# A seventh slot for weights, with three engines that prepare them one unit further on

## The reference

```
for layer in range(2):
    h = rmsnorm(x, g[0])
    m = mixer_ab(h, ...) if layer % 2 == 0 else mixer_cd(h, ...)
    x = x + rmsnorm(m, g[1])
    x = x + rmsnorm(cross_attn(rmsnorm(x, g[2]), mem, wq, wkv, wo), g[3])
    x = x + rmsnorm(sq_relu_mlp(rmsnorm(x, g[4]), w1, w2), g[5])

def mixer_cd(h, w_in, ...):               # layer 1
    u = h @ w_in                          # 5 x 1024 columns: a, gate, bg, cg, hh
    v = causal_dwconv(a * sigmoid(gate), dw_w) + dw_b       # 31 taps
    conf_out = silu(layernorm(v))
    sc_out = bg * causal_dwconv(cg * hh, sc_w)              # 3 taps
    return concat([conf_out, sc_out]) @ w_out
```

## Time and profile before

| | us |
|---|---|
| median of 3 runs | 913.75 (913.74 to 916.39) |
| profiled execution | 913.8, span 912.1 |
| PE busy | 882.5 (97% of the span) |
| DVE busy | 622.3 (68%) |
| ACT busy | 478.3 (52%) |
| POOL busy | 176.6 (19%) |

### The profile page before, as it was taken

One profiled execution on the slowest core, in us unless ns is written; L12 is line 12 of the kernel. 1 busy time (PEld: TensorE's weight loads), 2 busy tenths in 40 slices (PEclk: granted clock), 3 DMA queues, 4 the chain that ended last, 5 costly groups with the idle time before them and its releaser, 6 DMA issues.

```text
span 912.1 us, 14743 instructions
## 1 busy us (share of the span) xinstructions
PE 882.5 (97%) x6078; PEld 803.3 (88%) x6078; DVE 622.3 (68%) x960; ACT 478.3 (52%) x696; POOL 176.6 (19%) x163
## 2 busy tenths in 40 slices
PE   8999998999999999999998999999998899999997
PEld 8899986898899999998898998887997798999996
DVE  5886996586487555555579999956685565555554
ACT  6754654565465444444564443347664555444443
POOL 1120800000000000000019887666000000000000
PEclk9999999999999999999999999999999999999999
DMA  8554434544465555555556676255542456655551
GB/s 297 164 169 133 140 131 145 171 153 143 149 184 188 187 193 187 185 186 186 183 162 186 194 211 201 95 183 162 172 144 82 136 189 211 192 189 188 185 186 69
DMA packets 82955, 155.27 MB, mean 170 GB/s; under 512 B 6839, under 2 KB 8777, under 8 KB 82889
## 3 DMA queue, kind: packets, MB, share of 16 engines
q1 hardware_dynamic: 82776, 154.29, 52.2%
q10 hardware_dynamic: 112, 0.05, 0.0%
HBM read 152.11 MB, written 1.05 MB: 168 GB/s over the span
## 4 chain that ended last, share of the span: by engine, by line
PE 76%; DVE 13%; ACT 4%; POOL 2%; DMA 1%; SPq 1%; issue 1%; DVEq 0%; POOLq 0%; ACTq 0%
PE ps L556 13%; PE ps L558 13%; PE ps L557 13%; PE ps L623 10%; PE ps L625 10%; PE ps L624 10%; DVE w_lo L1499 4%; DVE ps L1839 2%; ACT w_hi L1094 1%; DVE cv L2018 1%; POOL w_lo L2142 1%; PE ps L681 1%; DVE xT L1778 1%; DMA raw<-in_ab_w_in 1%; DVE xc L1566 1%
## 5 line engine op out<-in xcount | busy, mean ns | idle before, releaser
L1094 ACT ACTIVATE w_hi<-raw 128x1024 fp32r<-128x1024 f32 x284 | 295.4, 1054 | 223.6 <-DMA raw<-in_mlp_w 135.9
L1499 DVE TENSOR_TENSOR w_lo<-raw,w_hi 128x1024 fp32r<-128x1024 f32 x238 | 287.1, 1227 | 129.0 <-ACT w_hi L1094 128.4
L556 PE MATMUL ps<-h_hi,w_hi 128*128 128x256 f32 x1120 | 315.7, 282 | 9.8 <-POOL w_lo L2142 5.9
L558 PE MATMUL ps<-h_hi,w_lo 128*128 128x256 f32 x1120 | 313.3, 280 | 0.0
L557 PE MATMUL ps<-h_lo,w_hi 128*128 128x256 f32 x1120 | 313.3, 280 | 0.0
L556 PEld LDWEIGHTS ps<-h_hi,w_hi 128*128 128x128 f32 x1120 | 212.0, 189 | 13.1 <-POOL w_lo L2142 6.6
L558 PEld LDWEIGHTS ps<-h_hi,w_lo 128*128 128x128 f32 x1120 | 213.2, 190 | 0.0
L557 PEld LDWEIGHTS ps<-h_lo,w_hi 128*128 128x128 f32 x1120 | 211.8, 189 | 0.6
L2171 POOL TENSOR_TENSOR rfac<-stat,mhalf 128x1 f32<-128x1 f32 (+2 forms) x18 | 16.6, 923 | 632.9 <-DVE stat L1752 515.4
L2142 POOL TENSOR_TENSOR w_lo<-raw,w_hi 128x1024 fp32r<-128x1024 f32 x46 | 114.6, 2516 | 23.1 <-ACT w_hi L1094 23.1
L623 PE MATMUL ps<-w_hi,r_hi 128*128 128x512 f32 x256 | 101.0, 395 | 0.0
(11 more groups left out here) (270 smaller groups left out, 1241.8 us busy)
## 6 DMA issues: line engine op xcount, KB each, us to landing
raw<-in_mlp_w SPq DMA_DIRECT2D x128, 512.0 KB, 3.7
raw<-in_cd_w_in SPq DMA_DIRECT2D x40, 512.0 KB, 3.9
raw<-in_xa_wkv SPq DMA_DIRECT2D x32, 512.0 KB, 3.7
raw<-in_ab_w_in SPq DMA_DIRECT2D x24, 512.0 KB, 4.6
raw<-in_xa_wq SPq DMA_DIRECT2D x16, 512.0 KB, 3.6
raw<-in_xa_wo SPq DMA_DIRECT2D x16, 512.0 KB, 3.7
raw<-in_cd_w_out SPq DMA_DIRECT2D x16, 512.0 KB, 3.5
raw<-in_ab_w_out SPq DMA_DIRECT2D x12, 512.0 KB, 3.4
```

The lines of the kernel that those rows point to most:

```text
L556: nc.tensor.matmul(dst, wt[0], x[0], start=start, stop=False, skip_group_check=True)
L558: return nc.tensor.matmul(dst, wt[1], x[0], start=False, stop=stop, skip_group_check=True)
L1094: nc.scalar.activation(w_hi[:, v % SLOTS, :, :], raw[:, v % SLOTS, :, :], ACT.Copy)\
L1499: V.tensor_tensor(w_lo[:, v % SLOTS, :, :], raw[:, v % SLOTS, :, :], f(w_hi[:, v % SLOTS, :, :]), ALU.subtract).then_inc(lo_ready_dve, 1)
```

## The change

SLOTS becomes 7, and the three while loops, on ACT, DVE and POOL, go one unit further than the number in the call for all calls from unit 7 on. [...] The places of the calls aren't edited. `v_at`, from which SP issues its copies of v, contains SLOTS and moves by one unit with it.

```
 P = 128
-SLOTS = 6
+SLOTS = 7
+AHEAD = 1
...
             def round_to(u):
 
-                while nu[0] <= min(u, NU - 1):
+                while nu[0] <= min(u + AHEAD if u >= SLOTS else u, NU - 1):
...
             def low_to(u):
 
-                while nu[0] <= min(u, NU - 1):
+                while nu[0] <= min(u + AHEAD if u >= SLOTS else u, NU - 1):
                     v = nu[0]
                     if not pool_lo[v]:
...
             def low_to(u):
 
-                while nu[0] <= min(u, NU - 1):
+                while nu[0] <= min(u + AHEAD if u >= SLOTS else u, NU - 1):
                     v = nu[0]
                     if pool_lo[v]:
...
-        nc = bacc.Bacc("TRN2", target_bir_lowering=False, num_devices=1)
+        nc = bacc.Bacc("TRN2", target_bir_lowering=False, num_devices=1, dynamic_dma_scratch_size=8192)
```

## The result

The changed kernel is slower: 918.82 us (median of 20 runs, 912.82 to 923.68) against 914.79 us (20 runs, 910.93 to 919.24) on the same chips. The ratio is 1.0046, with a 95% interval of 1.0029 to 1.0063. The profiled execution took 917.85 us, its span is 916.1 us (before 912.1), its mean granted clock 0.991 of full (before 0.994).

The account below looks back on a forecast made before the run. The prediction took TensorE, busy in 97% of the span, as the bound. It summed 1.3 us at the start and 4.5 in layer 1's projections to 5.8, so 913.8 became 908.0 us, with an 8-in-10 range of 904.9 to 911.3.

Parts of the forecast that it names:

- The start, 1.3 us: 0 to 136 us: TensorE's early waits shrink, but VectorE sets the pace; worth VectorE's lead, 1.3 us, between 0 and 3.7.
- The three therefore do the same work at the same moments and wait the same: Whole kernel: ScalarE, VectorE and GpSimd keep their timing; TensorE alone gains, a margin of 2.76 us.
- The waits near 480 us: Layer 1's projections: TensorE waits 0.9 us for unit 148, 1.0 for 149, then runs some 0.6 us ahead of before.
- The 1.38 us wait at 543.33 goes entirely: Layer 1's projections: the margin of 2.76 us removes this TensorE wait, leaving it 2.0 us ahead.
- 3.4 us ahead: Layer 1's projections, before 568.08: units 178/179 come earlier, 2.6 + 0.8 us, with about 1 us of wait left.
- The cap, 3.35 us of slack at S: End of layer 1's projections: VectorE's second sum, with at most 1.3 us of its own gain, caps the stage at 4.3 to 4.7 us.
- The clock fall at 569.5 gone: Layer 1's projections: TensorE's clock no longer falls after the shortened wait, 1.7 us more, 5.1 in all before the limit.
- The rest: From 600 us on: waits of 2.32 us at 691.30 and 3.23 us at 721.95 stay; no gain.
- The rival "slower": 476 to 596 us: VectorE meets GpSimd more often, 2.98 us per newly held group of taps; four give 919.8 us; chance 0.05.

Follow-up runs that it names:

- slots7_only: The kernel before with seven slots and the small scratch, every engine taking its units at the old places: 909.61 us, ratio 0.9949.
- dve_as_before: The changed kernel, but VectorE takes no unit further in the calls for units 140 to 199: 917.21 us, ratio 1.0060.
- pool_yields: The changed kernel, but GpSimd waits for VectorE's low part of unit u-1 before beginning its own of unit u: 912.48 us, ratio 0.9979.

## Why the prediction was wrong, step by step

- *The start, 1.3 us*: right in the first trace, 1.6 us at 478 us, and the new wait for cbm stands where it was named. In the second trace nothing of it is left: VectorE reaches Rsq at 474.24 us, before at 474.22. And the gain was put down to the two parts of the change together; the slot alone gives 2.2 us.
- *"The three therefore do the same work at the same moments and wait the same"*: this step failed. It holds for an engine that handles every unit. But VectorE and GpSimd share the units here, and with each call one unit further VectorE's own unit moves to an earlier call: that of 159 stood behind six taps at 507.00 and stands ahead of them at 503.76, and GpSimd's runs shift as well. What VectorE and GpSimd then hold each other up by was priced at nothing in the sum. It measured 7.2 us in low parts and 2.1 in ml in the profiled execution, 3.1 and 2.1 in the second trace. VectorE's chain grew by 8.4 and 4.4 us.
- *The waits near 480 us*: two of 0.9 and 1.0 us said, 0.76 and 1.55 found, so that the gain of 0.6 us didn't come. The second counted 1.28 us for GpSimd's multiplication of sg between the two low parts; that took 2.28, with VectorE's low part of 151 beside it.
- *"The 1.38 us wait at 543.33 goes entirely", "3.4 us ahead" at 568*: 1.10 us of the first stayed, and the second became 3.27 us. It depends on GpSimd's multiplication of cv, which waits for VectorE's fourth group of taps of cv (1.28 us, up to 565.72); that ended at 565.6 us, before at 561.4 (556.67 + 4.77).
- *The cap, 3.35 us of slack at S*: the sum is right, its sign wasn't. S ends at 600.21 + 2.45 = 602.66, 6.7 us later than 595.94; less the slack of 3.35 this is 3.4 us, which is what TensorE lost there (599.29 to 602.72). With the clock that fell behind the wait that makes some 5 us, of which 1 comes back by 695 us (695.37 for 691.30), and 4.0 remain between the spans.
- *The clock fall at 569.5 gone*: it stayed, behind a longer wait (3.27 us for 2.19). The 1.7 us counted for it are in no run as such: the shares of the earlier trace rows give them as an estimate, (0.05 + 0.29) x 5. What the trace of before shows is 16 intervals between matmuls from 569.45 to 572.82, at a granted clock of 0.50 from 570 to 572 us; after that they are 0.118 us, so these 3.37 us would have been 1.9, 1.5 less. Nor do waits of 1.99 us and less always leave the clock up: in `slots7_only` it fell behind one of 1.99 us (0.79 of full in 476 to 484 us) and not behind one of 2.19 (1.00 in 566 to 576).
- *The rest*: unchanged as said (2.34 and 3.23 us). That the wait at 691.30 is also for h_lo was half of it: both stood behind one rounding, and moving that took 1.6 us off.
- *The rival "slower"* named the two engines' holding each other up, and was given 0.05. It looked at the taps, whose 4.77 us are 4.88 now, and not at the low parts that the change itself moves. Its price per event, 2.98 us, was near the worst of them in the changed kernel (2.76), but one held operation can cost more than one such price: 10.4 us in `dve_as_before`.

Shown: that VectorE's operations on SBUF alone are held up beside GpSimd's (low parts up to 3.97 us for 1.22 in the changed kernel, ml 2.76 for 0.68), that a wait on GpSimd takes some of this away and is worth 4.7 us, and that with fills in place of GpSimd's subtractions they are short (the low part of 159 1.21 us, ml 0.69) and the changed kernel is the faster. Not settled: why a low part of VectorE beside an unbroken run of GpSimd's took 1.22 us in `slots7_only` and 11.60 in `dve_as_before`; where the 2.9 us between `pool_yields` and `slots7_only` go; and what else spreads the runs of one kernel over 5 us and more. Of the changed kernel's 20 runs the eight above 920 us show a granted clock of 0.986 to 0.990, the twelve below 0.990 to 0.993; whether hold-ups made the waits that the clock fell behind isn't shown, since the two traces are of runs below 918.

## What to carry to other kernels

More buffers and more looking ahead are two changes: the first makes data ready earlier (a ratio of 0.9949 here), the second also changes which work of two engines falls together (1.0046 with both); try them apart. Where VectorE and GpSimd both read SBUF, list for every moved VectorE operation what GpSimd does at that moment (low parts of 1.22 us took 3.97 and 11.60 here). Remember that units shared out between two engines move to other calls when the calls look further ahead. One trace shows one pattern of hold-ups; a second of the same kernel can show another (7.2 and 3.1 us here), so take two before you name one operation as the cause. A wait that makes GpSimd let a VectorE operation pass can be worth more than it costs (4.7 us less here), if TensorE needs the two results in that order anyway.

## What the runs showed that I had not expected

- A VectorE operation of 1.2 us can take 11.60 us beside GpSimd's subtractions when these follow each other without a pause; it need not (1.22 us in a run of ten). In that kernel the times of 12 runs fall into two groups, 914.4 to 917.3 and 924.3 to 926.5 us; the traced execution, 926.4 us, is of the upper one. That all of that group have such a stall is likely and not shown.
- GpSimd is held up too: its multiplication of cv takes 2.21 us where it meets a low part of VectorE (at 528.81 in before, with VectorE's at 528.65), 1.29 us elsewhere.
- TensorE issues matmuls of 256 columns at 113 or at 117 to 118 ns over long stretches, at the same granted clock (1.00) and in the same code; which it is differs between executions of one kernel, 427 or 443 in 50 us. Over some 60 us of these projections that is an estimated 2 us (60 x 16 / 443). Its cause stays open.
